# Value products of the second pair's attention, gathered by head and made in 64-column halves

## The reference

```
def dilated_pair(q, k, v, bias_tab, window, dil):       # a, three windows mixed by their sums
    ...
    p = jnp.exp(s - lse[..., None]).astype(v.dtype)
    o = jnp.einsum('bnrhqk,bnkrhd->bnqrhd', p, vb)
def diff_attention(q1, q2, k1, k2, v, lam, bias_tab):   # b, two softmaxes for each row
        a = probs(q1, k1) - lam * probs(q2, k2)
        return jnp.einsum('bhqk,bkhd->bqhd', a.astype(v.dtype), v)
def causal_attention(q, k, v):                          # c
        p = jax.nn.softmax(jnp.where(causal, s, -jnp.inf), axis=-1)
        return jnp.einsum('bhqk,bkhd->bqhd', p.astype(v.dtype), v)
```

## Time and profile before

| | |
|---|---|
| median of 3 runs | 1842.97 us (1841.17 to 1843.08) |
| the profiled execution | 1841.61 us, span 1839.8 us |
| TensorE matmuls busy | 98% of the span, its weight loads 88% |
| VectorE, ScalarE, GpSimd busy | 66%, 50%, 42% |
| the second pair's attention loop | 745.3 to 829.0 us and 1349.3 to 1433.0 us |

### The profile page before, as it was taken

One profiled execution on the slowest core, in us unless ns is written; L12 is line 12 of the kernel. 1 busy time (PEld: TensorE's weight loads), 2 busy tenths in 40 slices (PEclk: granted clock), 3 DMA queues, 4 the chain that ended last, 5 costly groups with the idle time before them and its releaser, 6 DMA issues.

```text
span 1839.8 us, 32454 instructions
## 1 busy us (share of the span) xinstructions
PE 1803.4 (98%) x12438; PEld 1616.9 (88%) x12438; DVE 1219.3 (66%) x2469; ACT 915.2 (50%) x1789; POOL 776.9 (42%) x601
## 2 busy tenths in 40 slices
PE   9999999999999999999999999999999999999997
PEld 7898888878898888888999998888888899999886
DVE  5797475379364363885999984266379589998533
ACT  4242276474366465873545443327487355454323
POOL 2533262255553354344443335544424344433652
PEclk9999999999999999999999999999999999999999
DMA  8444141123221232102232323222320223323321
GB/s 334 172 172 168 16 115 59 69 74 135 102 48 55 88 133 104 58 2 92 93 109 99 115 92 136 89 88 99 108 87 2 92 70 116 106 102 115 115 92 46
DMA packets 37029, 182.33 MB, mean 99 GB/s; under 512 B 8289, under 2 KB 9185, under 8 KB 18957
## 3 DMA queue, kind: packets, MB, share of 16 engines
q1 hardware_dynamic: 30664, 168.89, 26.6%
q10 hardware_dynamic: 6212, 11.36, 2.0%
HBM read 178.10 MB, written 5.41 MB: 100 GB/s over the span
## 4 chain that ended last, share of the span: by engine, by line
PE 86%; DVE 7%; ACT 4%; issue 2%; POOL 1%; DMA 1%; DVEq 0%; SPq 0%; ACTq 0%
PE ps L1665 17%; PE ps L1667 17%; PE ps L1666 17%; PE ps L2379 7%; PE ps L2381 7%; PE ps L2380 7%; PE ps L2285 3%; PE ps L1745 2%; PE ps L1759 2%; PE ps L2199 2%; PE ps L2303 2%; PE ps L1726 1%; POOL w_lo L874 1%; ACT pt L1131 1%; ACT w_hi L1004 1%
## 5 line engine op out<-in xcount | busy, mean ns | idle before, releaser
L874 POOL TENSOR_TENSOR w_lo<-raw,w_hi 128x512 fp32r<-128x512 f32 (+1 forms) x343 | 477.0, 1423 | 624.2 <-ACT w_hi L1004 624.0
L1004 ACT ACTIVATE w_hi<-raw 128x1024 fp32r<-128x1024 f32 (+3 forms) x174 | 170.9, 1025 | 226.0 <-PE ps L1667 209.1
L980 POOL TENSOR_TENSOR w_lo<-raw,w_hi 128x512 fp32r<-128x512 f32 x80 | 112.7, 1409 | 223.2 <-ACT w_hi L1069 223.0
L1665 PE MATMUL ps<-h_hi,w_lo 128*128 128x512 f32 (+1 forms) x496 | 177.2, 357 | 3.8 <-DVE h_lo L2468 3.7
L1666 PE MATMUL ps<-h_lo,w_hi 128*128 128x512 f32 (+1 forms) x496 | 174.5, 352 | 0.0
L1667 PE MATMUL ps<-h_hi,w_hi 128*128 128x512 f32 (+1 forms) x496 | 174.5, 352 | 0.0
L1665 PE MATMUL ps<-w_hi,hid_lo 128*128 128x512 f32 x352 | 137.1, 390 | 0.0
L1666 PE MATMUL ps<-w_lo,hid_hi 128*128 128x512 f32 x352 | 137.0, 389 | 0.0
L1667 PE MATMUL ps<-w_hi,hid_hi 128*128 128x512 f32 x352 | 136.9, 389 | 0.0
L2468 DVE TENSOR_TENSOR hid_lo<-hid,hid_hi 128x512 fp32r<-128x512 f32 x44 | 65.4, 1530 | 102.1 <-ACT hid_hi L1105 102.1
L1665 PE MATMUL ps<-w_hi,g_lo 128*128 128x512 f32 (+3 forms) x320 | 114.2, 357 | 1.5 <-POOL w_lo L874 1.3
(11 more groups left out here) (375 smaller groups left out, 5548.8 us busy)
## 6 DMA issues: line engine op xcount, KB each, us to landing
raw<-in_tiles SPq DMA_DIRECT2D x139, 1024.0 KB, 4.8
strips<-bias_rows ACTq DMA_DIRECT2D x18, 256.0 KB, 3.6
raw<-in_tiles SPq DMA_DIRECT2D x4, 832.0 KB, 4.1
bias_rows<-bias_row SPq DMA_DIRECT2D x10, 320.0 KB, 10.2
raw<-in_tiles SPq DMA_DIRECT2D x4, 768.0 KB, 5.2
res<-in_x SPq DMA_DIRECT2D x2, 1024.0 KB, 6.5
ln<-in_ln_g ACTq DMA_DIRECT2D x4, 512.0 KB, 3.5
ln<-in_ln_b ACTq DMA_DIRECT2D x4, 512.0 KB, 4.8
```

The costliest lines, as they stand in the source:

```text
L874: pool.tensor_tensor(w_lo[:, i % SPLIT, a:e], raw_of(what)[:, a:e], w_hi[:, i % SPLIT, a:e].bitcast(F32), ALU.subtract).then_inc(s_tile_lo ...
L980: pool.tensor_tensor(lo, quad_of(what[0], j, name), hi.bitcast(F32), ALU.subtract).then_inc(s_pool_piece.sem, s_pool_piece.nth(((what[0], ...
L1004: act.activation(w_hi[:, i % SPLIT, a:b], raw_of(what)[:, a:b], ACT.Copy).then_inc(s_tile_hi.sem, s_tile_hi.nth((what, n)))
L1665: pe.matmul(o, lhs[1], rhs[0], start=first, stop=False)
```

## The change

- The 64 ranks are put in 13 groups: the first four b ranks, then the four row blocks of one c or a head, with the one or two b ranks that fall between them. `mix(g)` makes all products of a group in one go, two turns after its last rank, into one of two banks (5 and 7) that serve for outputs alone. Each product is made as two halves of 64 queries: the stationary operand is 64 columns, the output lies on partitions 0 to 63 or 64 to 127.
- The last group is mixed after the first of the four steps of the first tile of the output projection.
- Turned probabilities have three banks instead of five; a bank is free once they are copied out.
- VectorE, not ScalarE, copies them for the 12 b ranks after group 0, at the end of its step.
- `rows_out2` acts once for a group: one reciprocal of four sums and one multiplication of 4x64 columns for the head's four row blocks, and a reciprocal and a scaling for each b rank in it.
- The copies go to more places: `pt_rows`, `pt_cos`, `pt_vc`, and the ring slot of the tile `up`. So the load that follows into that slot (the third tile after it, half of `w_o`) waits for the last group's product.

The core of the diff (left out: the new signals, the checks on the groups, the places where a wait for the rank's output becomes one for its group's):

```
-        pt2 = [at(f"pt2_{i}", [P, SEQ], names["g_hi"][0] + 4 * (C_HEADS + i) * SEQ) for i in range(2)]
-        pt2.append(at("pt2_2", [P, SEQ], names["cos2"][0]))
+        pt_rows = at("pt_rows", [P, 2 * SEQ], names["g_hi"][0] + 4 * C_HEADS * SEQ)
+        pt_cos = at("pt_cos", [P, SEQ], names["cos2"][0])
+        pt_vc = at("pt_vc", [P, 384], names["vc"][0] + names["vc"][1])
+        assert names["vc"][1] + 4 * 384 <= 4 * TILE
...
-        N_S, N_T, N_B, N_P = 3, 5, 5, 3
-        S_BANKS, T_BANKS = (4, 6, 0), (2, 1, 3, 5, 7)
+        N_S, N_T, N_B = 3, 3, 5
+        S_BANKS, T_BANKS, OUT_BANKS = (4, 6, 0), (2, 1, 3), (7, 5)
...
-        out_step = {what: turn_step[r + 3] if r + 3 <= LAST else STEPS for what, r in last_of.items()}
+        GROUPS, MIXED, group_of = [[]], {}, {}
+        for r, i in enumerate(RANKS):
+            if len(GROUPS) == 1 and len(GROUPS[0]) == XT or len([q for q in GROUPS[-1] if UNITS[RANKS[q]]["kind"] != "b"]) == XT:
+                GROUPS.append([])
+            GROUPS[-1].append(r)
...
+                u = UNITS[RANKS[r]]
+                if u["kind"] != "b":
+                    a = VW * u["i"]
+                elif g == 0:
+                    a = HD * u["i"]
+                else:
+                    a, singles = VW * XT + HD * singles, singles + 1
+                MIXED[r] = OUT_BANKS[g % 2], a
...
+        def pt_place(y, r):
+            u, landing = UNITS[RANKS[r]], raw_of((y, "up"))
+            if u["kind"] == "b":
+                where, a = ((pt_rows, 768), (landing, 1792), (pt_vc, 0), (landing, 1280))[u["i"]]
+            elif group_of[r] % 2 == 0:
+                where, a = landing, (1152, 896, 512, 0)[u["i"]]
+            else:
+                where, a = ((pt_rows, 640), (pt_rows, 384), (pt_rows, 0), (pt_cos, 0))[u["i"]]
+            return where[:, a:a + u["n"]]
+        def pt_free(r):
+            u = UNITS[RANKS[r]]
+            if u["kind"] == "b":
+                before = [group_of[q] for q in range(r) if UNITS[RANKS[q]]["kind"] == "b" and UNITS[RANKS[q]]["i"] == u["i"]]
+                return before[-1] if before else None
+            return group_of[r] - 2 if group_of[r] > 2 else None
+        def copied_by_vector(r):
+            return UNITS[RANKS[r]]["kind"] == "b" and group_of[r] > 0
+        ended = {what: GROUPS[group_of[r]][-1] for what, r in last_of.items()}
+        out_step = {what: turn_step[r + 3] if r + 3 <= LAST else STEPS for what, r in ended.items()}
...
                     else:
                         sp.wait_ge(s_tile_lo.sem, s_tile_lo.at(before))
+                    if before[1] == "up":
+                        sp.wait_ge(s_mixed.sem, s_mixed.at((before[0], len(GROUPS) - 1)))
...
-                        n = UNITS[RANKS[r]]["n"]
-                        act.wait_ge(s_turned.sem, s_turned.at((y, r)))
-                        if r >= N_P:
-                            act.wait_ge(s_mixed.sem, s_mixed.at((y, r - N_P)))
-                        act.activation(pt2[r % N_P][:, 0:n], ps[:, TURNED["unit", r], 0:n], ACT.Copy).then_inc(s_pt.sem, s_pt.nth((y, r)))
+                        if not copied_by_vector(r):
+                            act.wait_ge(s_turned.sem, s_turned.at((y, r)))
+                            if pt_free(r) is not None:
+                                act.wait_ge(s_mixed.sem, s_mixed.at((y, pt_free(r))))
+                            act.activation(pt_place(y, r), ps[:, TURNED["unit", r], 0:UNITS[RANKS[r]]["n"]], ACT.Copy).then_inc(s_pt.sem, s_pt.nth((y, r)))
                     if step == FROM:
...
-                def mix(r):
-
-                    u, b = UNITS[RANKS[r]], TURNED["unit", r]
-                    pe.wait_ge(s_pt.sem, s_pt.at((y, r)))
-                    if u["kind"] == "c":
+                def mix(g):
+
+                    kinds = {UNITS[RANKS[r]]["kind"] for r in GROUPS[g]}
+                    pe.wait_ge(*emptied[OUT_BANKS[g % 2]])
+                    emptied[OUT_BANKS[g % 2]] = s_o_out.after((y, g))
+                    if "c" in kinds:
                         pe.wait_ge(s_proj.sem, s_proj.at((y, "vc", XT - 1)))
                         pe.wait_ge(s_vc_ones.sem, s_vc_ones.at(y))
-                    if u["kind"] == "a":
+                    if "a" in kinds:
                         pe.wait_ge(s_va_ones.sem, s_va_ones.at(y))
-                    for j, v in enumerate(u["vs"]):
-                        m = pe.matmul(ps[:, b, 0:v.shape[1]], pt2[r % N_P][:, P * j:P * j + P], v, start=j == 0, stop=j == len(u["vs"]) - 1)
-                    m.then_inc(s_mixed.sem, s_mixed.nth((y, r)))
+                    for r in GROUPS[g]:
+                        u, (b, a), turned = UNITS[RANKS[r]], MIXED[r], pt_place(y, r)
+                        if copied_by_vector(r):
+                            pe.wait_ge(s_pt_b.sem, s_pt_b.at((y, r)))
+                        else:
+                            pe.wait_ge(s_pt.sem, s_pt.at((y, r)))
+                        for j, v in enumerate(u["vs"]):
+                            for half in (0, HD):
+                                m = pe.matmul(ps[half:half + HD, b, a:a + v.shape[1]], turned[:, P * j + half:P * j + half + HD], v,
+                                              start=j == 0, stop=j == len(u["vs"]) - 1)
+                    m.then_inc(s_mixed.sem, s_mixed.nth((y, g)))
 
...
+                        emptied[b] = s_pt_b.after((y, r)) if copied_by_vector(r) else s_pt.after((y, r))
                         for j in range(len(UNITS[i]["vs"])):
                             m = pe.transpose(ps[:, b, P * j:P * j + P], probs_of(i)[:, P * j:P * j + P], ident[:])
                         m.then_inc(s_turned.sem, s_turned.nth((y, r)))
-                        if r >= 2:
-                            mix(r - 2)
+                        if r - 2 in (group[-1] for group in GROUPS):
+                            mix(group_of[r - 2])
                     if step in turn_at:
                         turn_chunk(turn_at[step], TURNED["chunk", turn_at[step]])
...
-                                mix(LAST - 1 + k)
+                            if kh == 0 and t == 0 and k == 0:
+                                mix(len(GROUPS) - 1)
                         m.then_inc(s_mm.sem, s_mm.nth((y, "o", 0, t) if kh else (y, "o part", 0, t)))
...
                 def rows_out2(r):
 
-                    u = UNITS[RANKS[r]]
-                    total = recips[:, u["sum"]:u["sum"] + 1]
-                    if u["kind"] == "b":
-                        step(V.reciprocal(total, sums[:, u["sum"]:u["sum"] + 1]))
-                    dve.wait_ge(s_mixed.sem, s_mixed.at((y, r)))
-                    if u["kind"] != "b":
-                        step(V.reciprocal(total, ps[:, TURNED["unit", r], HD:VW]))
-                    V.tensor_scalar(ao[:, u["i"], u["col"]:u["col"] + HD], ps[:, TURNED["unit", r], 0:HD], recips[:, u["sum"]:u["sum"] + 1], None,
-                                    ALU.mult).then_inc(s_o_out.sem, s_o_out.nth((y, r)))
+                    g = group_of[r]
+                    if r != GROUPS[g][-1]:
+                        return
+                    b = OUT_BANKS[g % 2]
+                    singles = [] if g == 0 else [q for q in GROUPS[g] if UNITS[RANKS[q]]["kind"] == "b"]
+                    u = [UNITS[RANKS[q]] for q in GROUPS[g] if q not in singles][0]
+                    w = HD if g == 0 else VW
+                    rows = ps[:, b, 0:XT * w].rearrange("p (i d) -> p i d", d=w)
+                    s0 = u["sum"] - u["i"]
+                    totals = recips[:, s0:s0 + XT].unsqueeze(2)
+                    if g == 0:
+                        step(V.reciprocal(totals, sums[:, s0:s0 + XT].unsqueeze(2)))
+                    for q in singles:
+                        x = UNITS[RANKS[q]]
+                        V.reciprocal(recips[:, x["sum"]:x["sum"] + 1], sums[:, x["sum"]:x["sum"] + 1]).then_inc(s_b_recip.sem, s_b_recip.nth((y, q)))
+                    dve.wait_ge(s_mixed.sem, s_mixed.at((y, g)))
+                    if g > 0:
+                        step(V.reciprocal(totals, rows[:, :, HD:VW]))
+                    m = V.tensor_tensor(ao[:, :, u["col"]:u["col"] + HD], rows[:, :, 0:HD], totals.broadcast_to((P, XT, HD)), ALU.mult)
+                    for q in singles:
+                        m.then_inc(s_rows_part.sem, s_rows_part.nth((y, q)))
+                        x = UNITS[RANKS[q]]
+                        dve.wait_ge(s_b_recip.sem, s_b_recip.at((y, q)))
+                        m = V.tensor_scalar(ao[:, x["i"], x["col"]:x["col"] + HD], ps[:, b, MIXED[q][1]:MIXED[q][1] + HD],
+                                            recips[:, x["sum"]:x["sum"] + 1], None, ALU.mult)
+                    m.then_inc(s_o_out.sem, s_o_out.nth((y, g)))
 
                 for st in range(EARLY, STEPS):
...
                         scored(st)
+                    r = turns(st)
+                    if r is not None and copied_by_vector(r):
```

(35 more changed lines are left out.)

## The result

The changed kernel takes 1857.2 us (median of four runs, 1854.95 to 1861.95), the kernel before 1842.6: a ratio of 1.0084, 95% interval 1.0064 to 1.0105. It is slower by 14.7 us; 15.6 us faster was forecast. The profiled execution took 1861.95 us, with a span of 1859.8.

What follows compares the result with a forecast made beforehand. TensorE was taken to bound the loops, VectorE close behind. A layer: -10.2 products, -1.2 output wait, +2.5 chunks, +0.6 group 0, +0.5 bunching = -7.8 us; both -15.6, so 1827.4 us, range 1819.5 to 1838.

Steps and rivals of the forecast that it cites:

- The form and price of a half product: Value products in the attention loops: overlapping halves cost 0.0295 us per instruction, making products 10.2 us less a layer.
- The 0.25 us for each run: Value products on TensorE: each run of halves pays 0.25 us once, 3.2 us a layer for 13 groups.
- Bunching: Attention loop: a group holds TensorE 1.4 to 2.1 us in one go; costs 0.5 us a layer, bounds 0 and 2.5.
- Group 0: Loop start: products of the first four ranks no longer fill TensorE's early steps; 0.6 us a layer lost.
- The chunks' low part: Turns reusing a chunk's bank, three banks: TensorE waits 0.5 us for each of five chunks, 2.5 a layer, bounds 0 and 4.5.
- The sum: Both layers: -7.8 us each, -15.6 together, so 1826.0 us profiled and 1827.4 as the median.
- forecast loop (75.9): Attention loop of 83.7 us, shortened by the 7.8 us a layer that the forecast gained.
- Held load, last group: Output projection: third tile's load, issued 2.4 us after the loop, hidden with 6 us to spare; last group's move adds nothing.
- the forecast's last test: Between the attention loops: the prediction is wrong if that stretch grows.
- Rival (1): Part with b ranks: VectorE sets the pace; 5.1 us a layer gained, 1832.8 us; chance 0.20 with anything up to 1839.
- The forecast's own test: Attention loops: the prediction is wrong if TensorE waits more than 5 us a loop for VectorE.
- Rival (3): Value products: halves don't overlap here and cost 0.050 us each; 1853.6 us; chance 0.04.

Runs made afterwards that it cites:

- e8_ahead_of_waits_t4: Changed kernel with four turn banks, one output bank, and ready products made just ahead of b ranks' turns and at group ends: 1830.4 us, 0.9938 of the kernel before.
- e12_ahead_t3: Changed kernel, its three turn and two output banks kept, with ready products made just ahead of turns that would wait: 1844.3 us, 1.0016 of the kernel before.
- e1_whole: Changed kernel with each group's products whole (128 queries) instead of in two halves: 1885.6 us, ratio 1.023.

## Why the prediction was wrong, by its own steps

**The form and price of a half product: right.** 0.033 us an instruction at 2.4 GHz with what a run adds (1.31 us for 40). Products and turned ranks fell by 49.5 - 38.6 = 10.9 us a loop in the kernel with four banks, where the clock is full; -10.2 was forecast. The 0.25 us for each run came, too: 62 runs instead of 12 cost 8.3 us more in products (27.6 - 19.3) and 4.6 in what stands ahead of them (23.9 - 19.3), 0.26 a run. The rule of the Trainium skill ("TensorE: Matmul & The Clock Gate", LDWEIGHTS) that a load takes its columns at 1.2 GHz would give two halves, if their loads queue, the time of one whole. The rows disagree: 2 x 0.033 for two halves against 0.109 for one whole. In the kernel before, halves alone gave nothing, by the price of a run.

**Bunching, +0.5 us a layer (bounds 0 and 2.5): the step that failed.** It rested on no row. In the first loop TensorE waits 8.67 us for `pair` and 1.58 for a score bank (`small`), 10.3 of the 16.5; 1.3 of them stand ahead of the first run, so 8.9 us belong to this term. I wrote that VectorE has "up to three scored banks to eat from" during a run. It has next to none. Timeline of all engines in the kernel with four banks around its fourth run (775.91 to 777.93; the clock is full here and the copies are not in it):

```profile
776.61 0.42 DVE L2985 CUSTOM_DVE_ANT_0 sc<-ps,strips_g 128x256 f32<-128x256 f32 x1
...
779.23 0.69 DVE L2985 CUSTOM_DVE_ANT_0 sc<-ps,strips_g 128x512 f32<-128x512 f32 x1 [2.20 <-PE ps L2251]
779.97 0.72 ACT L1565 ACTIVATE sc<-sc,small 128x512 f32<-128x512 f32 x1 [2.39 <-DVE small L2985]
...
781.51 0.91 PE L2251 MATMUL ps<-kc,qc 96*128 96x384 f32 x2 [0.82 <-DVE small L2985]
```

One stored score goes at 776.61, then VectorE idles 2.20 us, for a score that TensorE makes only behind the run; ScalarE idles 2.39 for VectorE; and 3.6 us behind the run TensorE idles 0.82, for VectorE in its turn. It is a ring: score, VectorE, exponential, `pair`, turn. Fed evenly, it went round with 2.8 us of waits in the loop before; fed in bursts, whoever is starved can be late afterwards. The first run of the kernel after does it through the copy that waits for group 0's products (for under 2 us, by the forecast; it was 2.60):

```profile
754.79 0.69 DVE L3088 COPY raw<-ps 128x512 f32<-128x512 f32 x1 [2.60 <-PE ps L2345]
...
757.32 0.33 PE L2364 MATMUL ps<-ident,sc 128*128 128x128 f32 x1 [0.87 <-DVE sc L2995]
```

With four banks the two waits make 10.6 us, so the clock isn't their cause. All but the first begin 1.8 to 6.1 us behind the end of a run. The work totals (VectorE at "91%" was to be the danger) could not show it. In fact VectorE was busy for 64.5 of 93.4 us, 69%. The two causes that I had for such a wait, copies and outputs in VectorE's order, are ruled out; that it is the schedule of the products is shown by the kernels that change nothing else: `e8_ahead_of_waits_t4` against four banks alone, `e12_ahead_t3` against the kernel after.

**Group 0, +0.6 us a layer: the mechanism right, 1.3 us.** It is A2 at its barest. In the kernel before, the products of the first ranks stand ahead of a turn that needs `pair`; in the kernel after, that turn waits before any run was made (TensorE before, then after):

```profile
747.56 1.10 PE L2285 MATMUL ps<-vb,pt 128*128 128x64 f32 x8 [0.25 <-ACT pt L1549]
...
749.00 0.33 PE L2285 MATMUL ps<-vb,pt 128*128 128x64 f32 x2
749.14 0.42 PE L2199 MATMUL ps<-bk,bq 128*128 128x128 f32 x2
749.56 0.66 PE L2303 MATMUL ps<-ident,sc 128*128 128x128 f32 x4
```

```profile
751.62 0.66 PE L2364 MATMUL ps<-ident,sc 128*128 128x128 f32 x4 [1.32 <-DVE sc L2995]
```

No long run can have starved anyone there. `e8_ahead_of_waits_t4` has products again in that place, and waits 0.18 us.

**The chunks' low part, +2.5 us (bounds 0 and 4.5): the mechanism right, the size at its upper bound.** 4.4 us in the first loop, with a further 1.8 for ScalarE's exponential.

**The clock: no term at all.** The fall from 1.00 to 0.93 is worth 0.07 x 93.4 = 6.5 us in the first loop and 0.04 x 90.4 = 3.6 in the second. By the account, products, turned ranks, scores and chunks together cost 6.6 us more in the first loop than with four banks. Nothing in the trace of before shows a lower clock in the loops; I could only have named it as a price of new waits.

**The sum.** 17.5 us are missing between the forecast loop (75.9) and the first one (93.4): 11.3 from waits (16.5, where 2.8 - 1.2 + 3.6 = 5.2 was allowed for), 6.6 from the clock, and 0.7 the other way from products. That makes 17.2.

**Held load, last group: right.** The stretch between the loops takes 520.9 us, 0.6 more than before; by the letter of the forecast's last test it grew, by little beside the loops. The tile loads go out at 843.13, 2.3 us behind the loop's end (2.4 was forecast). ScalarE splits the third at +14.7 us and the fourth at +25.1, where it was +13.8 and +24.2, and what it waits for ahead of the fourth is TensorE, not a transfer; ahead of the third it doesn't wait at all. Timeline of ScalarE, then of SyncE's queue, in the kernel after:

```profile
855.45 2.00 ACT L1056 ACTIVATE w_hi<-raw 128x1024 fp32r<-128x1024 f32 x2
865.86 2.01 ACT L1056 ACTIVATE w_hi<-raw 128x1024 fp32r<-128x1024 f32 x2 [8.42 <-PE ps L1719]
```

```profile
843.13 18.84 SPq L901 DMA_DIRECT2D raw<-in_tiles  x4
```

**The rivals.** Rival (1) named the right kind of wait ("a new wait inside its order") and capped it by VectorE's busy share, 1832.8 us; the real one came with VectorE at 69% of the loop. The forecast's own test, "if TensorE waits more than 5 us a loop for VectorE", is what was seen: 14.7. Rival (3) gave 1853.6 us, the nearest number, by a mechanism that isn't there. No case held starvation with a clock that falls for it.

**What stays open.** How much of the 8.9 us comes from starved engines (A) and how much from steps without cover (A2). The traces show both, the idle VectorE in a run and the wait ahead of the first one, and the order that fills the waits mends both at once. Then, where the clock falls and where it doesn't. The low part's wait stands at the first fall, but it isn't the whole condition: in the kernel after the two loops have the same waits (16.5 us each) and clocks of 0.93 and 0.96, and with four banks a wait of 1.6 us (ahead of the turn at 749.94) brought no fall. Nor is it only little work ahead: in `e1_whole` TensorE was busy for 9.67 of the 10 us from 766 to 776, and behind a wait of 1.58 us the clock fell at 779. No kernel here varied that by itself. Last, what the 6 us of waits in the fastest kernel's loop would take; from 753.7 to 803.6, most of its part with b ranks, VectorE is busy for 42.8 of 49.9 us, 86%, as in the kernel before.

## What to carry to other kernels

When operations are gathered into runs on the engine that bounds a ring of engines, price the run by what the others have in stock when it begins, read from their timeline, and not by their busy share, and ask of each place that loses its work which wait it had covered. Put gathered work where the engine would wait anyway (here just ahead of the turn that waits for `pair`); it kept the cheap products and took away half of the waits. And look at the granted clock behind each new wait of TensorE: here it cost 6.6 us in a loop, beside 13.7 us of added waits.

## What the hardware showed that I had not expected

- The granted clock went to 0.50 in the middle of a loop in which TensorE was never idle for more than 1.8 us at a time; 64 half products took 3.60 us there, against 2.02 in the kernel with four banks.
- Whole fp32 products cost more in a long run than in short ones, 0.109 us an instruction against 0.085 to 0.105.
- A run of halves starts 0.09 us later behind the transposes ahead of it than whole products do (5.6 us a loop for 62 runs), beside what the runs cost themselves.
- A filler of 64 columns with a 128-column weight costs 0.11 us (120 in 13.1 us), as much as a transposed block with 128 moving columns (0.109 where a score follows): half the moving columns saved nothing.
